# Hybrid SSM and attention layer on one core: the product tanh·z plus z made by VectorE instead of GpSimd

## The chip, the cores and the metric

One core of a Trainium2 chip runs the whole kernel in one launch. The metric is device time in microseconds (us). PE is the matrix engine (PEld its weight loads), DVE is VectorE, ACT is ScalarE, POOL is GpSimd, SP only issues DMAs. The five engines run their own instruction streams and meet by semaphores alone: a wait holds up everything that stands behind it on its own engine.

## The reference, cut to what matters

One layer of a streaming encoder works on 592 tokens (64 of a sample stream, 16 meta tokens, 512 of a prompt). A half-weight SwiGLU comes first, then one input projection that feeds a Mamba-2 branch and an attention branch, then their gated sum and a second SwiGLU. The change touches the gate of the Mamba-2 branch:

```python
P = u @ w_in            # columns: [SSD z | SSD x,B,C | dt | q | k | v | forget | gates]
...
y, final = ssd_chunked(xs, dt, a, bm, cm, ssm_init)      # chunked scan
y = y[:, front:front + L] + lw['d_skip'][:, None] * xs
y = y.reshape(b, L, D_SSM) * jax.nn.silu(z)              # the gate
yg = y.reshape(b, L, SSM_GROUPS, D_SSM // SSM_GROUPS)
yg = yg * lax.rsqrt(jnp.mean(yg * yg, axis=-1, keepdims=True) + EPS)
```

silu(z) is computed as 0.5 · (tanh(z/2) + 1) · z.

## The kernel before, in words

**Tiles.** The 592 tokens stand in five token tiles of 128, 128, 128, 128 and 80 rows. Every large product is made of three matmuls, since weights and activations are split into a rounded part (`wh`, `xah`) and a remainder (`wl`, `xal`). The weights come by DMA into `raw`; ACT rounds them to `wh`, and POOL makes `wl = raw - wh` (L798) in the stretch that matters here, in quarters of 128x512.

**Stages.** First SwiGLU, then the mixing stage (the change is there), then the output projection, the second SwiGLU and a final norm. The mixing stage has four iterations (`i` = 0 to 3) of two groups each (`g` = 0 and 1); one group is 256 columns of the Mamba-2 branch. Its input projection comes in pieces of 256 weight columns, in the order of the list `MID` = z, x, bc, z, x, bc, v, q0, q1, k. The first z belongs to g=0, the second to g=1.

**Order of the work.** There is no scheduler. One list of steps, written by hand, is shared by all engines: `FIRST_STEPS`, then `LOOP_STEPS` three times, then `LAST_STEPS`. Each engine has its own function `mid` that walks the list and does its part of every step. A step ("lin", n, t, ...) is PE's piece: token tile t of column piece n. It carries inner steps, placed between PE's 24 matmuls of the piece; `flat` hands an engine the inner steps first and the piece itself after them. So what DVE or POOL does for a piece stands in its stream behind what it does for the inner steps of that piece.

**Where the z pieces lie.** Five z tiles of g=0 open the stage (`FIRST_STEPS`, the "opening"). In each iteration the scan of g=0 (`ssd_window` with g=0: conv, then per token tile `s1`, `s1b`, `s2`) is run between the pieces z, x, bc of g=1, so the five z tiles of g=1 lie beside the scan of g=0. The scan of g=1 runs between v, q, k, with no z. In iterations 0 to 2 the attention heads (`heads_window`) run between the pieces z, x, bc of g=0 for the next iteration. That makes 5 + 4·5 + 3·5 = 40 z tiles.

**One z tile before the change.** PE makes the piece (`token_tile`, L1705); ACT evacuates it twice from PSUM: `zt` = tanh(z/2) and `zr` = z (L1076 and L1077 in the opening, L1079 and L1080 elsewhere), and raises `act_free`. Both have two buffers, so that ACT waits on `z_used` for the tile two back. POOL waits for `act_free` and makes `zt + 1` in place (L816), then `zs = zt · zr` (L817), and raises `z_used`. `zs` holds all five tiles of both groups; DVE reads it in `yg = 0.5 · y1 · zs` (L1586) at the end of a token tile's `s2`.

**DVE's part of the scan, by lines.** `s1`: four decay differences `eb` (L1539), which ACT turns into exponentials. `s1b`: `cbm` (L1546), the masked product C·B out of PSUM bank 5, and `mb` (L1550). `s2`: the states `sfin` or `spr` (L1563 to L1570), `y` (L1577, L1580, L1582), `yg` (L1586). PE writes C·B of the next token tile into the same bank (L1945), so that it waits until `cbm` of the tile before has been read:

```python
pe.wait_ge(cbm_ready, i * 10 + (PRIMED + tau))                       # s1 on PE
pe.matmul(bank(5, m, m), cv[:, 2, c], cv[:, 3, c], start=True, stop=True).then_inc(cb_ready, 1)
```

**The opening on DVE.** Eight norm products `full` (L1451) and eight remainders `xal` (L1455), in inner steps of the z pieces, then the small chain of the step sizes (L1461 to L1480) whose result `tstack` PE transposes (L1761).

**POOL's other work in the mixing stage** is `wl` (L798), the columns of the conv's history, and in `s1` the three products `xdd`, `xsk`, `xd` per token tile (L839).

Of the kernel before, what the change touches and what calls it, by code (L numbers as in the profile page):

```python
# [8 lines left out]
ALU = mybir.AluOpType  # L9
# [35 lines left out]
ROWS = [128, 128, 128, 128, TOK - 512]  # L45
# [63 lines left out]
PRIMED = 2  # L109


MID = ["z", "x", "bc", "z", "x", "bc", "v", "q0", "q1", "k"]
# [176 lines left out]
def freed(i, n, t):  # L289


    return i * MID_OUTS + (KT + 1 + OUT_AT[n] + t + 1)
# [28 lines left out]
def fox_ssd_hybrid_kernel(nc, x_prompt, x_sample, cache_k, cache_v, cache_logf, state_ssm, state_conv,  # L321
# [6 lines left out]
    with ctx:  # L328
# [80 lines left out]
        with ExitStack() as s:  # L409
# [12 lines left out]
            zt = sb("zt", [P, 2, 256], F32, s)  # L422
            zr = sb("zr", [P, 2, 256], F32, s)
            zs = sb("zs", [P, 2, TILES, 256], F32, s)
# [52 lines left out]
        hi_ready, split_done, key_split = sem("hi_ready"), sem("split_done"), sem("key_split")  # L477
        cleared = sem("cleared")
        lin_out, act_free, dve_free = sem("lin_out"), sem("act_free"), sem("dve_free")
        gated, full_ready, xhi_ready, x_ready = sem("gated"), sem("full_ready"), sem("xhi_ready"), sem("x_ready")  # L480
        sq_ready, sq_used, ss_ready, ss_summed = sem("sq_ready"), sem("sq_used"), sem("ss_ready"), sem("ss_summed")
        root_ready, rs_ready, a_ready, sc_ready = sem("root_ready"), sem("rs_ready"), sem("a_ready"), sem("sc_ready")
# [6 lines left out]
        z_used, hist_ready = sem("z_used"), sem("hist_ready")  # L489
        tap0_ready, taps_done, tanh_ready, cv_done = sem("tap0_ready"), sem("taps_done"), sem("tanh_ready"), sem("cv_done")  # L490
        brow_in, sraw_in, sraw_T, sini_ready = sem("brow_in"), sem("sraw_in"), sem("sraw_T"), sem("sini_ready")
        dec_ready, cst_T, cst_ready, cst_out = sem("dec_ready"), sem("cst_T"), sem("cst_ready"), sem("cst_out")
        xb_T, xb_ready, cb_ready, cbm_ready = sem("xb_T"), sem("xb_ready"), sem("cb_ready"), sem("cbm_ready")
        seg_ready, e_ready, m_ready, xd_ready = sem("seg_ready"), sem("e_ready"), sem("m_ready"), sem("xd_ready")
        xdd_ready = sem("xdd_ready")
        st_ready, s_ready, yo_ready, yd_ready = sem("st_ready"), sem("s_ready"), sem("yo_ready"), sem("yd_ready")
        y_used, yg_ready, sq_done, rv_ready = sem("y_used"), sem("yg_ready"), sem("sq_done"), sem("rv_ready")
# [6 lines left out]
        qk_ready, s_free, p_ready, p_T = (sem(n) for n in ("qk_ready", "s_free", "p_ready", "p_T"))  # L504
# [216 lines left out]
        def _(pool):  # L721
# [3 lines left out]
            def link(ins):  # L725
                ins.then_inc(gch, 1)
                pool.wait_ge(gch, chain.up())

            def settle():

                pool.sem_inc(passed, 1)

            pool.sem_inc(z_used, PRIMED)


            def input_half(n):

# [65 lines left out]
            def mid(now, steps):  # L803
                for step in flat(steps):
                    i, kind, g = now, step[0], step[1] if len(step) > 1 else 0
                    if kind == "split":
                        split_quarter(1 - MID_SLOT[g], step[2], split_cols(g), shared(g, step[2]))
                    if kind == "lin" and MID[g] == "z":

                        i, t, g = now + step[3], step[2], g // 3  # L810
                        if t == 0 and step[3]:
                            pool.wait_ge(yg_ready, now * 10 + (PRIMED + 5))
                        m, b = ROWS[t], (g + t) % 2
                        pool.wait_ge(act_free, freed(i, step[1], t))
                        settle()
                        link(pool.tensor_scalar(zt[0:m, b, :], zt[0:m, b, :], 1.0, None, ALU.add))  # L816
                        pool.tensor_tensor(zs[0:m, g, t, :], zt[0:m, b, :], zr[0:m, b, :], ALU.mult).then_inc(z_used, 1)  # L817
                    elif kind == "lin" and MID[g] == "x" and step[2] == 0:

                        i, g = now + step[3], g // 3  # L820
                        pool.wait_ge(taps_done, i * 8 + (PRIMED + 4 * g))
                        pool.wait_ge(cst_T, i * 2 + (PRIMED + g))
                        settle()
                        hist = par[:, PC_STATE:PC_STATE + 96].rearrange("p (r t) -> p t r", r=3)
                        pool.memset(xp[:, :, CS_ + SAMPLE:CP_], 0.0)
                        pool.tensor_copy(xp[:, 0:2, 0:3], hist[:, bass.ds(i * 4 + 2 * g, 2), :])
                        pool.tensor_copy(xp[:, 2:3, 0:3], hist[:, bass.ds(i * 2 + (16 + g), 1), :])
                        pool.tensor_copy(xp[:, 3:4, 0:3], hist[:, bass.ds(i * 2 + (24 + g), 1), :]).then_inc(hist_ready, 1)
                    elif kind == "s1":
                        t = step[2]  # L830
                        m, b, hs, tau = ROWS[t], (t + g) % 2, i * 8 + 4 * g, PRIMED + 5 * g + t
                        xv = xbt[0:m, b, 0:256].rearrange("p (h c) -> p h c", h=4)
                        pool.wait_ge(xb_ready, i * 10 + (tau + 1))
                        pool.wait_ge(yd_ready, i * 10 + (tau - 1))
                        pool.wait_ge(y_used, i * 10 + (tau - 1))


                        def by_column(dst, src):
                            return pool.tensor_tensor(dst[0:m, b, :].rearrange("p (h c) -> p h c", h=4), xv,  # L839
                                                      src.unsqueeze(2).to_broadcast([m, 4, HD]), ALU.mult)  # L840

                        by_column(xdd, tokt[0:m, t, bass.ds(hs + 64, 4)]).then_inc(xdd_ready, 1)
                        by_column(xsk, dsk[0:m, bass.ds(hs, 4)])
                        by_column(xd, tokt[0:m, t, bass.ds(hs + 32, 4)]).then_inc(xd_ready, 1)
                    elif kind == "fetch":
                        pool.wait_ge(ssd_left, i + 1)
                        settle()
                        pool.memset(pp[:, :, 0:SAMPLE], 0.0).then_inc(pz_ready, 1)
                    elif kind == "stage":
                        pool.wait_ge(heads_left, 4 + g)  # L850
                        settle()
                        k0, k1 = ((0, 3), (3, KT))[g]
                        to = 0
                        for c0, c1 in KEPT:
                            pool.dma_start(G2["h"][:, k0:k1, to:to + c1 - c0], oa_spill[k0:k1, :, c0:c1].rearrange("j p t -> p j t"))\
                                .then_inc(stage_in[g], 16)
                            to += c1 - c0
# [412 lines left out]
        def _(dve):  # L1270
# [2 lines left out]
            chain, full, xhi, nsplit = Count(), Count(), Count(), Count()  # L1273
            half = HALF

            for s in (split_done, dve_free, a_ready, full_ready, taps_done, cv_done, seg_ready, cbm_ready, m_ready, s_ready, y_used, yg_ready, s_free):
                dve.sem_inc(s, PRIMED)

            def link(ins):
# [136 lines left out]
            def stage(i, n):  # L1416

                k = n - 2
                if k >= 0:
                    hh, t = job(k)  # L1420
                    m = ROWS[t]
                    dve.wait_ge(pv_ready, i * JOBS + (k + 1))
                    link(dve.reciprocal(rinv[0:m, k % 4:k % 4 + 1], rsum[0:m, k % 4:k % 4 + 1]))
                    dve.tensor_scalar(otok[0:m, t, HD * hh:HD * hh + HD], bank(7, HD, m, at=256),
                                      rinv[0:m, k % 4:k % 4 + 1], None, ALU.mult).then_inc(o_ready, 1)
                if n < JOBS:
                    hh, t = job(n)
                    m, (before, w) = ROWS[t], score_span(t)
                    dve.wait_ge(bias_in[hh % 2], i * 96 + 48 * (hh // 2 + 1))
                    diagonal = bias[0:m, hh % 2, PAST:PAST + m] if t == 0 else bias[0:m, hh % 2, PAST + P + before:PAST + P + w]  # L1430
                    link(dve.tensor_tensor(diagonal, diagonal, negmask[0:m, min(t, 1), 0:m], ALU.add))
                    dve.wait_ge(qk_ready, i * JOBS + (n + 1))
                    if n >= 2:
                        dve.wait_ge(p_T, i * JOBS + (n - 1))
                    bs = bias[0:m, hh % 2, 0:PAST + P] if t == 0 else bias[0:m, hh % 2, PAST + P:PAST + P + w]
                    dve.sem_inc(met, 1)
                    dve.tensor_tensor_reduce(out=scores(t), in0=bank(4, w, m, at=BANK - before), in1=bs, scale=1.0, scalar=LEAST,
                                             op0=ALU.add, op1=ALU.min, accum_out=mx[0:m, n % 4:n % 4 + 1]).then_inc(s_free, 1)

            def mid(now, steps):  # L1440
                for step in flat(steps):
                    i, kind, g = now, step[0], step[1] if len(step) > 1 else 0
                    if kind == "half" and g % 2 == 0:
                        stage(i, g // 2)
                    elif kind == "norm":

                        if g < KT:
# [81 lines left out]
                    elif kind == "s1":  # L1529
                        t = step[2]  # L1530
# [549 lines left out]
```

## Time and profile before

| what | value |
|---|---|
| median of 3 runs | 2035.76 us (2035.05 to 2035.95) |
| profiled execution, its own time | 2037.11 us |
| its span | 2035.5 us |
| granted clock of PE | 0.994 of full speed |
| PE busy | 1980.0 us, 97% of the span |
| DVE busy | 988.7 us, 49% |
| ACT busy | 754.9 us, 37% |
| POOL busy | 425.7 us, 21% |

The profiled execution took 1.35 us more than the median of the runs; its span, from the first to the last instruction, is 1.6 us shorter than its own time. Shares of busy time are averages over stages that differ.

### The profile page before, as it was taken

The page shows a single profiled execution, that of the slowest core. Times are in us where ns is not written, and L with a number is a line of the kernel's source. Part 1 is how long each engine was busy: PE and PEld are TensorE (multiplying, and loading weights), DVE is VectorE, ACT ScalarE, POOL GpSimd, SP SyncE. Part 2 cuts the span into 40 slices and gives each one's busy share as a digit, 9 for nine tenths or more (in the row PEclk, how much of TensorE's full clock was granted, in tenths as well). Part 3 has the DMA queues.
Part 4 walks back from the last instruction along what each step waited for, and adds up shares of the span by engine and source line. Part 5 has one row for each costly group of instructions (what it writes and reads, how often), then busy time and mean ns, then how long its engine had stood idle before and what let it go on. Part 6 is the DMA issues. An engine that isn't in the chain of part 4 may idle for free. (4 is left out here: it accounts for less than half of the span.)

```text
span 2035.5 us, 36914 instructions
## 1 busy us (share of the span) xinstructions
PE 1980.0 (97%) x14807; PEld 1929.5 (95%) x14807; DVE 988.7 (49%) x1713; ACT 754.9 (37%) x1362; POOL 425.7 (21%) x516
## 2 busy tenths in 40 slices
PE   6999999998999999999999999999999999999997
PEld 6999999997899989998999899999999999999997
DVE  4433432457873477347735872214454543343344
ACT  5221221235455445554555454333223322222223
POOL 1000000005644264416442643223110000000000
PEclk9999999999999999999999999999999999999999
DMA  5222222213325222522261225315433222222222
GB/s 155 64 87 77 82 83 83 72 56 111 94 86 174 66 73 68 177 63 81 60 200 41 81 62 166 104 54 161 130 105 107 83 83 89 77 82 89 77 67 62
DMA packets 226657, 190.04 MB, mean 93 GB/s; under 512 B 10880, under 2 KB 214976, under 8 KB 225376
## 3 DMA queue, kind: packets, MB, share of 16 engines
q1 hardware_dynamic: 221568, 173.76, 28.4%
q0 software_dynamic: 4416, 14.32, 2.3%
q8 instruction: 88, 1.44, 0.3%
q14 instruction: 41, 0.34, 0.1%
q10 hardware_dynamic: 544, 0.17, 0.0%
HBM read 168.89 MB, written 19.33 MB: 92 GB/s over the span
## 5 line engine op out<-in xcount | busy, mean ns | idle before, releaser
L1693 PE MATMUL ps<-xah,wh 128*128 128x296 f32 (+1 forms) x2336 | 516.8, 302 | 6.9 <-DVE xal L1298 3.9
L1693 PE MATMUL ps<-xah,wl 128*128 128x296 f32 (+1 forms) x2336 | 515.4, 302 | 0.0
L1693 PE MATMUL ps<-xal,wh 128*128 128x296 f32 (+1 forms) x2336 | 510.2, 300 | 0.0
L1693 PEld LDWEIGHTS ps<-xah,wh 128*128 128x128 f32 x2336 | 378.4, 190 | 8.6 <-DVE xal L1298 3.5
L1693 PEld LDWEIGHTS ps<-xal,wh 128*128 128x128 f32 x2336 | 379.8, 189 | 0.0
L1693 PEld LDWEIGHTS ps<-xah,wl 128*128 128x128 f32 x2336 | 377.6, 189 | 0.1
L798 POOL TENSOR_TENSOR wl<-raw,wh 128x512 fp32r<-128x512 f32 (+1 forms) x184 | 231.4, 1265 | 412.5 <-ACT wh L917 412.5
L1693 PE MATMUL ps<-xbl,wh 128*128 128x288 f32 (+1 forms) x1312 | 282.6, 297 | 0.0
L1693 PE MATMUL ps<-xbh,wh 128*128 128x288 f32 (+1 forms) x1312 | 281.1, 295 | 1.1 <-DVE xbl L1292 1.1
L1693 PE MATMUL ps<-xbh,wl 128*128 128x288 f32 (+1 forms) x1312 | 280.7, 295 | 0.0
L909 ACT ACTIVATE wh<-raw 128x2048 fp32r<-128x2048 f32 x84 | 160.1, 1906 | 243.1 <-PE ps L1693 243.1
L1286 DVE TENSOR_TENSOR wl<-raw,wh 128x2048 fp32r<-128x2048 f32 x85 | 194.9, 2293 | 103.9 <-ACT wh L909 91.1
L1693 PEld LDWEIGHTS ps<-xbh,wl 128*128 128x128 f32 x1312 | 212.8, 190 | 0.0
L1693 PEld LDWEIGHTS ps<-xbh,wh 128*128 128x128 f32 x1312 | 210.6, 188 | 1.3 <-issue 1.3
L1693 PEld LDWEIGHTS ps<-xbl,wh 128*128 128x128 f32 x1312 | 209.7, 188 | 0.0
L1338 DVE TENSOR_TENSOR full<-ps,rs 128x592 f32<-128x592 f32 (+1 forms) x44 | 33.7, 766 | 225.2 <-PE ps L1693 225.1
L1705 PE MATMUL ps<-wh,xal 128*128 128x256 f32 (+1 forms) x440 | 128.0, 291 | 0.0
L1705 PE MATMUL ps<-wh,xah 128*128 128x256 f32 (+1 forms) x440 | 125.6, 285 | 1.2 <-ACT zr L1080 1.2
L1705 PE MATMUL ps<-wl,xah 128*128 128x256 f32 (+1 forms) x440 | 124.9, 284 | 0.0
L1327 DVE SCALAR_TENSOR_TENSOR h<-ps,h 128x592 f32 (+3 forms) x56 | 42.8, 764 | 159.1 <-PE ps L1693 158.9
L917 ACT ACTIVATE wh<-raw 128x512 fp32r<-128x512 f32 (+1 forms) x192 | 110.4, 591 | 0.2
L1511 DVE SCALAR_TENSOR_TENSOR cvt<-xp,parh,cvt 128x595 f32<-128x595 f32 x96 | 98.5, 1026 | 19.7 <-ACT cvt L1145 17.9
(273 smaller groups left out, 2438.9 us busy)
## 6 DMA issues: line engine op xcount, KB each, us to landing
raw<-in_ffn_w_in_dram SPq DMA_DIRECT2D x88, 512.0 KB, 5.0
raw<-in_w_in_dram SPq DMA_DIRECT2D x80, 512.0 KB, 4.7
raw<-in_ffn_w_out_dram SPq DMA_DIRECT2D x32, 512.0 KB, 4.0
brow<-acs_rows SPq DMA_DIRECT2D x8, 1184.0 KB, 6.7
raw<-in_w_br_ssm_dram SPq DMA_DIRECT2D x16, 512.0 KB, 4.0
raw<-in_ffn_w_out_dram SPq DMA_DIRECT2D x16, 384.0 KB, 3.5
bias<-bias_rows SPq DMA_DIRECT2D x32, 160.0 KB, 5.2
os_spill<-yT SPq DMA_DIRECT2D x8, 592.0 KB, 3.0
```

The source lines that it names most:

```text
L798: ins = pool.tensor_tensor(wl[:, slot, k, 0:cols], raw[:, slot, k, 0:cols], wh[:, slot, k, 0:cols].bitcast(F32), ALU.subtract)
L909: act.activation(wh[:, slot, :, 0:cols], raw[:, slot, :, 0:cols], ACT.Copy).then_inc(hi_ready, 1)
L917: act.activation(wh[:, slot, k, 0:cols], raw[:, slot, k, 0:cols], ACT.Copy).then_inc(hi_ready if c == 3 else hi_part, 1)
L1286: dve.tensor_tensor(wl[:, slot, :, 0:cols], raw[:, slot, :, 0:cols], wh[:, slot, :, 0:cols].bitcast(F32), ALU.subtract)\
L1327: dve.scalar_tensor_tensor(out=hm, in0=halves(b, half=half), scalar=0.5, in1=hm, op0=ALU.mult, op1=ALU.add)\
L1338: link(dve.tensor_tensor(in_halves(G["full"][:, n, :]), halves(4 * n + 2, half=half), rs, ALU.mult))
L1511: ins = dve.scalar_tensor_tensor(out=c, in0=xp[:, j, tap:tap + CO], scalar=parh[:, bass.ds(conv_tile(i, g, j) + 32 * tap, 1)], in1=c, op0= ...
L1693: ins = pe.matmul(bank(b + a, half), w[:, slot, k, j * P:(j + 1) * P], x[:, k, a * half:(a + 1) * half], start=(k == 0 and w is wh and x i ...
L1705: ins = pe.matmul(bank(b, 256, m), x[:, k, t * P:t * P + m], w[:, slot, k, :], start=(k == 0 and w is wh and x is xh), stop=(k == KT - 1 a ...
```

## The change

POOL no longer touches z. DVE makes `zs = (zt + 1) · zr` in one scalar_tensor_tensor per tile, in its own branch of `mid` for the z pieces, and raises `z_used`, which is now primed by DVE.

```diff
@@ POOL
-            pool.sem_inc(z_used, PRIMED)
...
-                    if kind == "lin" and MID[g] == "z":
-
-                        i, t, g = now + step[3], step[2], g // 3
-                        if t == 0 and step[3]:
-                            pool.wait_ge(yg_ready, now * 10 + (PRIMED + 5))
-                        m, b = ROWS[t], (g + t) % 2
-                        pool.wait_ge(act_free, freed(i, step[1], t))
-                        settle()
-                        link(pool.tensor_scalar(zt[0:m, b, :], zt[0:m, b, :], 1.0, None, ALU.add))
-                        pool.tensor_tensor(zs[0:m, g, t, :], zt[0:m, b, :], zr[0:m, b, :], ALU.mult).then_inc(z_used, 1)
-                    elif kind == "lin" and MID[g] == "x" and step[2] == 0:
+                    if kind == "lin" and MID[g] == "x" and step[2] == 0:
@@ DVE
-            for s in (split_done, dve_free, ..., s_free):
+            for s in (split_done, dve_free, ..., s_free, z_used):
                 dve.sem_inc(s, PRIMED)
...
                     if kind == "half" and g % 2 == 0:
                         stage(i, g // 2)
+                    elif kind == "lin" and MID[g] == "z":
+
+                        i, t, g = now + step[3], step[2], g // 3
+                        m, b = ROWS[t], (g + t) % 2
+                        if t == 0 and step[3]:
+                            dve.wait_ge(yg_ready, now * 10 + (PRIMED + 5))
+                        dve.wait_ge(act_free, freed(i, step[1], t))
+                        dve.scalar_tensor_tensor(out=zs[0:m, g, t, :], in0=zt[0:m, b, :], scalar=1.0, in1=zr[0:m, b, :],
+                                                 op0=ALU.add, op1=ALU.mult).then_inc(z_used, 1)
```

In the changed kernel the new instruction is L1440, and the DVE lines named above come 3 earlier in the file (L1539 is L1536 there). The order of POOL's remaining work, of PE's and of ACT's is the same.

**DVE in the opening, before** (norm products and remainders of the first steps; `rsb_ready` is the norm's root, `xhi_ready` ACT's rounded part):

```order
L1451 TENSOR_TENSOR full<-h,rs 128x592 [waits rsb_ready] x2
L1455 SCALAR_TENSOR_TENSOR xal<-full,par,xah 128x592 [waits xhi_ready]
L1451 TENSOR_TENSOR full<-h,rs 128x592 [waits x_ready,rsb_ready]
L1455 SCALAR_TENSOR_TENSOR xal<-full,par,xah 128x592 [waits xhi_ready]
L1451 TENSOR_TENSOR full<-h,rs 128x592 [waits x_ready,rsb_ready]
L1455 SCALAR_TENSOR_TENSOR xal<-full,par,xah 128x592 [waits xhi_ready]
```

The same place in the changed kernel:

```order
L1440 SCALAR_TENSOR_TENSOR zs<-zt,zr 128x256 [waits act_free]
L1448 TENSOR_TENSOR full<-h,rs 128x592 [waits rsb_ready] x2
L1452 SCALAR_TENSOR_TENSOR xal<-full,par,xah 128x592 [waits xhi_ready]
L1440 SCALAR_TENSOR_TENSOR zs<-zt,zr 128x256 [waits act_free]
L1448 TENSOR_TENSOR full<-h,rs 128x592 [waits x_ready,rsb_ready]
L1452 SCALAR_TENSOR_TENSOR xal<-full,par,xah 128x592 [waits xhi_ready]
L1440 SCALAR_TENSOR_TENSOR zs<-zt,zr 128x256 [waits act_free]
L1448 TENSOR_TENSOR full<-h,rs 128x592 [waits x_ready,rsb_ready]
```

A z product that waits for ACT now stands ahead of the first norm product, and one between each group of them.

**DVE in the scan of g=0 (one iteration), before**, from the end of the conv to the states of token tile 0 (`cv` is the conv's output, `m_ready` DVE's own earlier `mb`, `cb_ready` PE's C·B, `e_ready` ACT's exponentials, `st_ready` PE's states):

```order
L1526 SCALAR_TENSOR_TENSOR cv<-th,cvt 128x64 [waits tanh_ready]
L1526 SCALAR_TENSOR_TENSOR cv<-th,cvt 128x528
L1539 TENSOR_SCALAR eb<-brow,tokt 128x128 [waits m_ready,heads_left,brow_in]
L1539 TENSOR_SCALAR eb<-brow,tokt 128x128 x3
L1546 TENSOR_TENSOR cbm<-ps,mask 128x128 [waits cb_ready]
L1550 TENSOR_TENSOR mb<-eb,cbm 128x512 [waits yd_ready,e_ready,cbm_ready]
L1539 TENSOR_SCALAR eb<-brow,tokt 128x128 [waits m_ready]
L1539 TENSOR_SCALAR eb<-brow,tokt 128x128 x3
L1563 SCALAR_TENSOR_TENSOR sfin<-sini,dec,ps 128x64 [waits sini_ready,sf_T,dec_ready,st_ready]
```

The same place in the changed kernel:

```order
L1440 SCALAR_TENSOR_TENSOR zs<-zt,zr 128x256 [waits act_free]
L1523 SCALAR_TENSOR_TENSOR cv<-th,cvt 128x64 [waits tanh_ready]
L1523 SCALAR_TENSOR_TENSOR cv<-th,cvt 128x528
L1440 SCALAR_TENSOR_TENSOR zs<-zt,zr 128x256 [waits act_free]
L1536 TENSOR_SCALAR eb<-brow,tokt 128x128 [waits m_ready,heads_left,brow_in]
L1536 TENSOR_SCALAR eb<-brow,tokt 128x128 x3
L1543 TENSOR_TENSOR cbm<-ps,mask 128x128 [waits cb_ready]
L1547 TENSOR_TENSOR mb<-eb,cbm 128x512 [waits yd_ready,e_ready,cbm_ready]
L1440 SCALAR_TENSOR_TENSOR zs<-zt,zr 128x256 [waits act_free]
L1536 TENSOR_SCALAR eb<-brow,tokt 128x128 [waits m_ready]
L1536 TENSOR_SCALAR eb<-brow,tokt 128x128 x3
L1560 SCALAR_TENSOR_TENSOR sfin<-sini,dec,ps 128x64 [waits sini_ready,sf_T,dec_ready,st_ready]
```

The z products of token tiles 1 and 2 now stand ahead of the `eb` of token tiles 0 and 1, which waited for nothing of ACT's before; that of tile 0 stands ahead of the conv's last part.

## Rows read from the trace of the kernel before

**Rows 1.** The page's first part: busy time of each engine, share, instructions.
```profile
PE 1980.0 (97%) x14807; PEld 1929.5 (95%) x14807; DVE 988.7 (49%) x1713; ACT 754.9 (37%) x1362; POOL 425.7 (21%) x516
```
**Rows 2.** PE's waits, whole span: line, what it waited for, us, times, longest.
```profile
PE ps L1945 <- DVE cbm L1546: 7.7, 8, 1.4
PE ps L1761 <- DVE tstack L1480: 5.8, 1, 5.8
PE ps L1693 <- POOL wl L798: 3.0, 1, 3.0
```
**Rows 3.** Single lines: duration in ns (min/median/max), first and last start in us.
```profile
L816 POOL TENSOR_SCALAR zt<-zt x40: 843/856/1372, 475.3 to 1151.7; 128x256 f32<-128x256 f32 x32, 80x256 f32<-80x256 f32 x8
L817 POOL TENSOR_TENSOR zs<-zt,zr x40: 724/733/984, 476.3 to 1152.7; 128x256 f32<-128x256 f32 x32, 80x256 f32<-80x256 f32 x8
L1586 DVE SCALAR_TENSOR_TENSOR yg<-y,zs x40: 420/572/1945, 543.6 to 1222.5; 128x256 f32<-128x256 f32 x32, 80x256 f32<-80x256 f32 x8
L1582 DVE TENSOR_TENSOR y<-y x40: 420/442/1011, 542.9 to 1222.0; 128x256 f32<-128x256 f32 x32, 80x256 f32<-80x256 f32 x8
```
**Rows 4.** Scans of g=0, g=1: us; busy PE, PEld, DVE, ACT, POOL; clock; DMA; GB/s.
```profile
526.76:576.36 49.60, 46.27 (x347) 43.09 (x345) 40.15 (x94) 25.92 (x63) 29.55 (x38) 1.00 0.25 76
586.66:632.70 46.04, 45.45 (x347) 43.07 (x346) 35.26 (x90) 23.18 (x56) 19.86 (x26) 1.00 0.27 81
```
**Rows 5.** The opening: two lines' durations, then timeline rows (start, us; idle before).
```profile
L1451 DVE TENSOR_TENSOR full<-h,rs x8: 764/954/1680, 473.0 to 489.8; 128x592 f32<-128x592 f32 x8
L1455 DVE SCALAR_TENSOR_TENSOR xal<-full,par,xah x8: 833/1324/1872, 475.8 to 491.4; 128x592 fp32r<-128x592 f32 x8
...
472.99 2.18 DVE L1451 TENSOR_TENSOR full<-h,rs 128x592 f32<-128x592 f32 x2 [5.66 <-ACT rs L1109]
490.49 2.24 DVE L1455 SCALAR_TENSOR_TENSOR xal<-full,par,xah 128x592 fp32r<-128x592 f32 x2
474.65 0.47 ACT L1077 ACTIVATE zr<-ps,rcol 128x256 f32<-128x256 f32 x1
```
**Rows 6.** Timeline of DVE, scan of g=0, iteration 0.
```profile
534.18 1.02 DVE L1539 TENSOR_SCALAR eb<-brow,tokt 128x128 f32<-128x128 f32 x4
536.21 0.29 DVE L1546 TENSOR_TENSOR cbm<-ps,mask 128x128 f32<-128x128 f32 x1 [1.02 <-PE ps L1945]
538.05 2.49 DVE L1539 TENSOR_SCALAR eb<-brow,tokt 128x128 f32<-128x128 f32 x4
541.05 0.85 DVE L1563 SCALAR_TENSOR_TENSOR sfin<-sini,dec,ps 128x64 f32<-128x64 f32 x4 [0.51 <-PE ps L1965]
544.28 0.28 DVE L1546 TENSOR_TENSOR cbm<-ps,mask 128x128 f32<-128x128 f32 x1
545.41 2.31 DVE L1539 TENSOR_SCALAR eb<-brow,tokt 128x128 f32<-128x128 f32 x4
```
**Rows 7.** Timeline of ACT and POOL beside it.
```profile
535.50 0.36 ACT L1080 ACTIVATE zr<-ps 128x256 f32<-128x256 f32 x1
536.90 0.63 ACT L917 ACTIVATE wh<-raw 128x512 fp32r<-128x512 f32 x1
538.50 0.38 ACT L1080 ACTIVATE zr<-ps 128x256 f32<-128x256 f32 x1
...
535.82 1.28 POOL L798 TENSOR_TENSOR wl<-raw,wh 128x512 fp32r<-128x512 f32 x1
```
**Rows 8.** Timeline of PE beside it: C·B of token tiles 2, 3 and 4.
```profile
544.74 0.39 PE L1945 MATMUL ps<-cv 128*128 128x128 f32 x2
550.65 0.49 PE L1945 MATMUL ps<-cv 128*128 128x128 f32 x2 [0.52 <-DVE cbm L1546]
557.06 0.37 PE L1945 MATMUL ps<-cv 128*80 128x80 f32 x2 [1.38 <-DVE cbm L1546]
```
**Rows 9.** Heads window of iteration 0: busy times as in rows 4, DVE's longest wait.
```profile
642.90:726.50 83.60, 83.21 (x650) 77.40 (x649) 37.37 (x113) 44.32 (x105) 23.65 (x26) 1.00 0.39 117
DVE bias L1431 <- DMA bias<-biasp_rows: 22.1, 1, 22.1
```

More of the change, by code:

```diff
@@ L1274, in _ @@
             half = HALF
-            for s in (split_done, dve_free, a_ready, full_ready, taps_done, cv_done, seg_ready, cbm_ready, m_ready, s_ready, y_used, yg_ready, s_free):
+            for s in (split_done, dve_free, a_ready, full_ready, taps_done, cv_done, seg_ready, cbm_ready, m_ready, s_ready, y_used, yg_ready, s_free, z_used):
                 dve.sem_inc(s, PRIMED)
```

## Prediction, made before the changed kernel was run

> **What bounds the kernel now.** The busy times come first: PE works 97% of the span, DVE 49%, POOL 21% [rows 1]. Neither DVE nor POOL bounds the whole; either can cost time only where PE waits for it. So the second view is PE's waits [rows 2]. Two of them belong to DVE streams that the change alters: 7.7 us on `cbm` before C·B (L1945, 8 waits, up to 1.4 us) and 5.8 us on `tstack` at the end of the opening. One 3.0 us wait on POOL's `wl` lies in the opening too, ahead of the one on `tstack`; whatever is won there is waited again, so it counts nothing.
>
> The third view is the windows [rows 4]. The scan of g=0, with the z pieces of g=1 beside it, lasts 49.60 us; the scan of g=1, with no z, 46.04. Its PE work is the same in number (347 matmuls each). The difference of 3.56 us is what z with its company costs today in one scan, and there are four of them. PE is idle 49.60 - 46.27 = 3.33 us in the first, 0.59 us in the second. The rest of the argument is about the order of DVE's stream there.
>
> The fourth is the durations [rows 3, 5]. An instruction of DVE with two inputs in SBUF has a steady shortest time and a wide spread: `yg` 420 ns alone, up to 1945. `eb` took 1.02 us for four in one place and 2.49 and 2.31 in two others [rows 6]; POOL ran `wl` or products at those two places, z's 843 and 724 ns among them. So the two engines hold each other up, and POOL's z costs DVE time although DVE does not do it.
>
> **The change part by part.** Durations are from the profiled execution.
>
> *POOL's 80 instructions go*: 40 x (0.856 + 0.733) = 63.6 us of POOL [rows 3]. POOL is 21% busy [rows 1], so the time itself is worth nothing. What it gives is less contention on DVE, counted below.
>
> *DVE gets 40 fused products.* The nearest row is `yg`, the same form and size: 0.42 us alone [rows 3]; 40 x 0.42 = 16.8 us. A rule of the Trainium skill speaks against that: Vector Engine (DVE) Microarchitecture Reference, section Points that are easy to get wrong, says that scalar_tensor_tensor with two SBUF sources that aren't bf16 runs at half throughput. The trace does not bear it out: `yg` in this form has the same shortest time as the plain tensor_tensor `y`, 420 ns for 256 elements [rows 3]. By the rule, with the streaming part of 256 elements doubled, the product would be about 0.7 us, 0.28 x 5 = 1.4 us more per scan and some 7 us over all.
>
> *The semaphores* (`z_used` raised by DVE, primed by it): nothing; ACT waits for the tile two back, a whole piece of 24 matmuls earlier. The `yg_ready` wait for the first tile is on DVE's own earlier work: nothing.
>
> *The opening, 5 tiles.* DVE starts its norm products at 472.99 today and ends the last remainder at 490.49 + 2.24 = 492.73 [rows 5]: 19.7 us for 8 + 8 instructions whose shortest times add up to 8 x 0.764 + 8 x 0.833 = 12.8 us [rows 5]. The 6.9 us between are port waits and one wait on ACT. With the change the first product waits for ACT's `zr`, which ends at 474.65 + 0.47 = 475.12; it ends at about 475.6, so the chain starts 2.6 us later. Then come 12.8 us, four more products of 0.42 (1.7 us), and the stretching that stays, W. The end is 475.6 + 12.8 + 1.7 + W = 490.1 + W. With W as today (6.9) that is 497.0, or +4.3; with W = 2.0 it is 492.1, or -0.6. POOL's z falls away but its `wl` quarters stay, and each later product stands at a place where ACT has just evacuated, about 1 us each. I take W = 4.1, so **+1.5 us**. PE waits 5.8 us at the end of this chain [rows 2], so all of it counts.
>
> *The scan of g=0, four times.* Five products stand in DVE's stream, and two of them ahead of work on the way to PE:
> - That of token tile 1 stands ahead of the first `eb`. Today `eb` starts at 534.18, before `zr` of tile 1, which ends at 535.50 + 0.36 = 535.86 [rows 6, 7]. POOL's `wl` starts at 535.82 and runs 1.28 us, to 537.10 [rows 7]. So the product ends at about 537.5 and `eb` at 538.5 with 1.0 us of its own, not at 535.20: **3.3 us late**.
> - ACT's exponential stands behind it, and behind that the `wh` quarter (today 536.90) and the evacuation of z tile 2 (today 538.50) [rows 7]. ACT had some slack there; they slip by about 1.6 to 2.2 us, so `zr` of tile 2 is ready near 540.7, its product at 541.2.
> - The second `eb` follows. It takes 2.49 us today, with POOL's z and other products beside it [rows 6]; I take 2.1 us, so its end is 543.3, not 540.54. `sfin`, today at 541.05, starts at about 543.2: **2.1 us late** [rows 6].
> - From there DVE is packed until the C·B of tile 4: `cbm` of tile 1 (today 544.28) comes at about 546.4, and PE's C·B of tile 2, at 544.74 today without a wait, waits for it, some 1.9 us. For tiles 3 and 4 PE waits 0.52 and 1.38 today [rows 8], behind the same chain.
> - Given back: the `eb` of tile 2 takes 2.31 us today [rows 6] and has no POOL z beside it after the change, about 1.0 us less; against it stands one more product. A product costs 0.42 and POOL's z of one tile held the port 1.6 us, so per tile up to 0.5 us comes back. From tile 2 to the 1.38 us wait of tile 4 that leaves about 1.1 us of the 2.1.
>
> So **+1.1 us per scan, +4.4 us in all**. The bounds: if the whole 3.56 us by which this window is longer went away and only the late start of 2.1 us came in, -1.5 us per scan, -6; if nothing were given back and a further wait for ACT stood in tile 3, +3 us per scan, +12.
>
> *The heads windows, 15 tiles.* DVE is busy 37.4 of 83.6 us, and its one long wait, 22.1 us, is on a DMA [rows 9]. PE is busy 83.21 of the 83.60. The products are hidden in DVE's idle time: **0**. If that cover were gone it would be 15 x 0.42 = 6.3 us.
>
> **Sum:** 1.5 + 4.4 + 0 = +5.9 us. The profiled execution took 2037.1 us, so 2043.0. It stood 1.35 us above the median of the runs; on the median the forecast is **2041.7 us**, 0.3% slower. About 0.2%, 4.1 us, is what a measurement of this kernel can tell from no change.
>
> **The rivals.**
> 1. *No change that can be told.* The late `eb` is absorbed: DVE's first `cbm` waits 1.02 us for PE today [rows 6], and the chain from tile 1 to tile 4 makes the loss up at 0.5 us per tile or more. Then +0.3 us per scan and +0.5 in the opening, 1.7 us in all: 2037.5. For it: PE's idle time in the scan is 3.33 us and only waits on `cbm` tie it to this chain [rows 4, 8]. Against it: PE's waits on `cbm` grow already today from tile 3 to tile 4, so DVE does not make time up there.
> 2. *Faster: the port binds the scan of g=0.* DVE is busy 40.15 us there against 35.26 without z, though it does four instructions more [rows 4]: some 4 us of its stretching are POOL's doing. If that is the cause of the 1.38 us wait, freeing the port shortens every token tile by more than the late start costs: -1.5 us per scan, -0.6 in the opening, 2029.2. It decides at the second `eb`: this case holds if it ends before about 541 and `cbm` of tile 1 starts no later than 544.6. For it: the tile periods of DVE's packed stretch hold 1.3 us of stretched `eb`. Against it: the first `eb` has to wait for `zr`, whatever the port does. By itself: the Trainium skill, GPSIMD Engine Reference, section Engine selection, puts additions and products of a tile on VectorE, GpSimd being about twice as slow with two inputs. The rows agree on the price (724 against 420 ns), but the rule says nothing of the place in the stream.
> 3. *Clearly slower: the products wait for ACT at every tile.* ACT evacuates z behind an exponential that itself waits for DVE's `eb`, so that the two engines alternate and nothing is given back: +2.5 us per scan and +3 in the opening, 13 us: 2048.8. For it: two of the products stand right behind such evacuations. Against it: from tile 3 on, ACT's evacuation comes before DVE reaches the place.
> That the change doesn't do what it says is no case: the 40 instructions stand in DVE's stream, and POOL's are gone.
>
> **How the numbers follow.** The forecast (+2.5 to +9 us, centre +5.9) 0.48, rival 1 0.27, rival 2 0.15, rival 3 0.10. The range takes in the forecast, rival 1 and the nearer half of each of the outer two: 2032.0 to 2048.5. Slower by over 0.2% is nearly all of the forecast (0.44) with rival 3 (0.10), 0.54; within 0.2% is rival 1 (0.27) with the forecast's low end (0.04), 0.31; faster 0.15.
>
> **What the profile would show.** Right: PE's wait on `tstack` grows from 5.8 to about 7.3 us; the g=0 window grows from 49.60 to about 50.7 while the g=1 window stays at 46.04; the first `eb` of a scan starts about 3 us later in it, behind a product that waited for `zr`; waits on `cbm` rise from 7.7 to about 12 us and appear at tile 2; the product's shortest time is 0.42 us; the heads windows stay as they are. Wrong: a g=0 window under 49 us (rival 2), a product of 0.7 us (the page's rule), growing heads windows (then DVE's idle time there was no cover), or a granted clock below today's in the scans.

## The result: slower by 0.7%, nearly all of it in the scans of g=0

| | median of the runs | profiled execution | span | granted clock |
|---|---|---|---|---|
| before (6 runs) | 2035.78 us (2035.05 to 2036.37) | 2037.11 | 2035.5 | 0.994 |
| changed (6 runs) | 2049.82 us (2047.85 to 2052.35) | 2050.47 | 2048.9 | 0.991 |

The ratio is 1.0067, 95% interval [1.0057, 1.0077]: 14 us slower, in the direction of the forecast (+5.9) but above its range. The page's first part of the changed kernel, to be read against [rows 1]:

```profile
PE 1985.9 (97%) x14807; PEld 1933.8 (94%) x14807; DVE 996.0 (49%) x1753; ACT 755.4 (37%) x1362; POOL 360.4 (18%) x436
```

POOL lost 65 us (63.6 forecast). DVE gained 7, less than the 16.8 of its products, so its other work took some 9 us less. But PE, whose 14807 matmuls are the same, is busy 5.9 us longer. Its waits, against [rows 2]:

```profile
PE ps L1942 <- DVE cbm L1543: 14.6, 8, 1.9
PE ps L1758 <- DVE tstack L1477: 7.3, 1, 7.3
PE ps L1690 <- POOL wl L796: 1.3, 1, 1.3
```

The wait on `tstack` grew by the 1.5 us that were forecast; those on `cbm` by 6.9. The windows of the two scans of iteration 0, in the columns of [rows 4]:

```profile
527.54:580.42 52.88, 48.01 (x347) 44.61 (x345) 41.01 (x99) 25.93 (x63) 21.77 (x27) 0.97 0.23 71
590.71:636.80 46.09, 45.47 (x347) 43.13 (x346) 35.28 (x90) 23.18 (x56) 19.83 (x26) 1.00 0.27 81
```

The scan of g=1 has not changed. The scan of g=0 takes 52.88 us against 49.60: 3.28 us more, where 1.1 were forecast. PE's idle time there is 52.88 - 48.01 = 4.87 us against 3.33, +1.5; its busy time is 48.01 against 46.27, +1.7, and the clock column has fallen to 0.97. The other three scans of g=0 grew as much (the table in the third set of runs).

The timeline of DVE in that scan:

```profile
534.75 0.42 DVE L1440 SCALAR_TENSOR_TENSOR zs<-zt,zr 128x256 f32<-128x256 f32 x1 [1.31 <-ACT zr L1068]
536.68 0.67 DVE L1440 SCALAR_TENSOR_TENSOR zs<-zt,zr 128x256 f32<-128x256 f32 x1 [0.75 <-ACT zr L1068]
537.27 1.98 DVE L1536 TENSOR_SCALAR eb<-brow,tokt 128x128 f32<-128x128 f32 x4
...
541.01 1.09 DVE L1440 SCALAR_TENSOR_TENSOR zs<-zt,zr 128x256 f32<-128x256 f32 x1 [0.32 <-ACT zr L1068]
542.02 1.97 DVE L1536 TENSOR_SCALAR eb<-brow,tokt 128x128 f32<-128x128 f32 x4
543.91 0.84 DVE L1560 SCALAR_TENSOR_TENSOR sfin<-sini,dec,ps 128x64 f32<-128x64 f32 x4
...
547.57 0.28 DVE L1543 TENSOR_TENSOR cbm<-ps,mask 128x128 f32<-128x128 f32 x1
...
549.35 0.86 DVE L1536 TENSOR_SCALAR eb<-brow,tokt 128x128 f32<-128x128 f32 x4
...
554.01 2.15 DVE L1536 TENSOR_SCALAR eb<-brow,tokt 128x128 f32<-128x128 f32 x4
...
559.65 0.28 DVE L1543 TENSOR_TENSOR cbm<-ps,mask 128x128 f32<-128x128 f32 x1
```

The scan began 0.8 us later than before (PE's first transpose of the conv's output at 536.22, before at 535.43), so 0.8 is to be taken off. The first `eb` ends at 537.27 + 1.98 = 539.25 (before 535.20): 3.3 us late, as forecast. Behind it ACT's `zr` of tile 2 is ready at 540.98 (before 538.88), 1.3 us late where 1.8 were forecast. `sfin` starts 543.91 - 541.05 - 0.8 = 2.1 us late, as forecast. `cbm` of tile 1 starts 547.57 - 544.28 - 0.8 = 2.5 us late. PE's side, C·B of tiles 2, 3 and 4 as in [rows 8]:

```profile
547.90 0.49 PE L1942 MATMUL ps<-cv 128*128 128x128 f32 x2 [1.86 <-DVE cbm L1543]
553.24 0.39 PE L1942 MATMUL ps<-cv 128*128 128x128 f32 x2
559.99 0.47 PE L1942 MATMUL ps<-cv 128*80 128x80 f32 x2 [1.83 <-DVE cbm L1543]
```

C·B of tile 2 now waits 1.86 us, that of tile 4 1.83 instead of 1.38. What follows the second wait is in the windows of 1 us (columns as in [rows 4]; the clock is the third from the end):

```profile
557.00:558.00 1.00, 1.00 (x10) 0.88 (x8) 0.96 (x3) 0.35 (x1) 0.57 (x1) 1.00 0.00 0
558.00:559.00 1.00, 0.15 (x2) 0.00 (x0) 0.98 (x1) 0.49 (x1) 0.95 (x2) 1.00 0.00 0
559.00:560.00 1.00, 0.01 (x1) 0.01 (x1) 0.95 (x3) 0.00 (x0) 1.00 (x2) 1.00 0.00 0
560.00:561.00 1.00, 1.00 (x5) 1.00 (x6) 0.96 (x2) 0.00 (x0) 1.00 (x2) 0.56 0.00 0
561.00:562.00 1.00, 1.00 (x4) 0.82 (x3) 0.79 (x4) 0.17 (x1) 0.22 (x1) 0.50 0.06 16
562.00:563.00 1.00, 1.00 (x5) 0.82 (x5) 0.22 (x2) 1.00 (x4) 0.00 (x0) 0.50 0.00 0
563.00:564.00 1.00, 1.00 (x8) 1.00 (x8) 0.64 (x4) 0.21 (x1) 0.71 (x1) 0.74 0.67 208
```

PE idles, and then, for some 3.5 us, its clock is granted at the lower level, 1.2 GHz, with half the matmuls to the microsecond. The shares missing add up to 0.44 + 0.50 + 0.50 + 0.26 = 1.7 us. Each of the four scans of g=0 has one such stretch in the changed kernel; none has one before.

The theory to be tested: the product is cheap, its **place** is not. It makes DVE wait for ACT ahead of work that PE waits for, and the longer waits bring the clock down. The main rival: it is the **price**, DVE having no room for five more instructions in a scan, wherever they stand.

### The profile page after: what moved, and what is told of

Same layout as the page of the kernel before. It is cut to its first block and busy times, and to the rows that moved or that the text cites. A ratio compares the mean times of both kernels' runs of the same rounds, so it can differ in the third digit from the quotient of the medians.

```text
span 2048.9 us, 36834 instructions
## 1 busy us (share of the span) xinstructions
PE 1985.9 (97%) x14807; PEld 1933.8 (94%) x14807; DVE 996.0 (49%) x1753; ACT 755.4 (37%) x1362; POOL 360.4 (18%) x436
## 3 DMA queue, kind: packets, MB, share of 16 engines
q1 hardware_dynamic: 221568, 173.76, 28.1%
```

## The experiments

### First set: which of the three places, and the same work one piece later

Three kernels make only the z tiles of one place on DVE, those of the others on POOL as before. The edit is against the kernel before; `on_dve` returns `steps is FIRST_STEPS` for the opening, `step[1] == 3` for the scans and `step[3] == 1` for the heads:

```diff
@@ POOL
-                    if kind == "lin" and MID[g] == "z":
+                    if kind == "lin" and MID[g] == "z" and not on_dve(now, step, steps):
...
@@ DVE
+                    elif kind == "lin" and MID[g] == "z" and on_dve(now, step, steps):
...
```

> Only the five z tiles of the opening are made by DVE, the other 35 by POOL as before. Place theory (a product that waits for ACT stands ahead of DVE's work on the way to PE): the chain up to tstack ends about 1.5 us later, PE's wait on tstack 7 to 7.5 us against 5.8; net about +1.5 us, 2037.3; the scans stay at 49.60 us with full granted clock. Price theory (DVE has no room for the products wherever they stand): 5/40 of the loss of 14 us, about +1.8 us. The two agree here; the run sizes the opening.

Measured: 2038.13 us against 2036.07 before on the same chip, ratio 1.0011 [1.0002, 1.002]: +2.1 us. PE waits 7.3 us on `tstack`.

> Only the 20 z tiles beside the scans of g=0 are made by DVE, the others by POOL as before. Place theory: nearly all of the loss, four times 3.3 us, about 2049 us; each scan of g=0 52.9 us long against 49.60, with about 1.5 us more idle time of PE and a stretch of some 3.5 us at half the granted clock. Price theory: half of the products, half of the loss, about 2043.

Measured: 2048.93 us, ratio 1.0061 [1.0048, 1.0075]: +12.9 us, with four stretches at half clock.

> Only the 15 z tiles beside the attention heads are made by DVE. Place theory: no change within 0.5 us of before (2035.8), since DVE waits there for DMA and PE. Price theory: 15/40 of the loss, about +5 us, 2041.

Measured: 2036.13 us, ratio 1.0 [0.9991, 1.0009]: no change that can be told. The three add up to 15.0 us, about the 14 of the whole. An equal share per product, as the simple price theory has it, is out: 20 products cost 12.9 us, 15 others nothing.

The fourth kernel keeps all 40 products on DVE, each one piece later in its stream (this edit and those that follow are against the changed kernel, but for `before_fill`):

```diff
-                    elif kind == "lin" and MID[g] == "z":
...
+                    elif kind == "lin":
+                        for held_now, held in late_z:
+                            z_product(held_now, held)      # the wait and the product as in the change
+                        late_z[:] = [(now, step)] if MID[g] == "z" else []
```

> All 40 tiles on DVE in the fused form, but each product stands one piece later in DVE's stream (behind the inner steps of the next piece), where ACT's evacuation has long ended. Same number of instructions and same price. Place theory: the scans' waits on cbm fall to those of before or below (7.7 us or less), no stretch at half clock in a scan, and the opening's chain starts as early as before: 2030 to 2036.5 us, that is as fast as before or a little faster since POOL's 1.6 us per tile no longer hold DVE up. Price theory: still 2045 to 2050.

Measured: 2034.48 us, ratio 0.9992 [0.9983, 1.0001]. The 14 us are gone with no product less. Its waits on `cbm` are under those of before, and its C·B of tiles 2 and 4 in iteration 0:

```profile
PE ps L1948 <- DVE cbm L1549: 6.6, 8, 1.1
```

```profile
542.60 0.49 PE L1948 MATMUL ps<-cv 128*128 128x128 f32 x2 [0.61 <-DVE cbm L1549]
...
554.24 0.37 PE L1948 MATMUL ps<-cv 128*80 128x80 f32 x2 [1.06 <-DVE cbm L1549]
```

So the place decides. That POOL's 64 us were taken off and the time hardly fell is not explained by this run; the third set shows it.

### Second set: which product, the clock, and the price

> The changed kernel, but beside the scans the products of token tiles 0 and 1 stand one piece later in DVE's stream; tiles 2 to 4, the opening and the heads stand as in the change. If the products ahead of the conv's last part and of the first eb are what counts (DVE's first eb starts 2.6 us later into the scan, ACT's evacuation of tile 2 slips behind it), the second product finds zr of tile 2 ready near its old time, C·B of tile 2 waits less than 1 us and the clock holds: 2036 to 2039 us, of which about 2 are the opening's. If the product ahead of the second eb is what counts, 2045 or more.

```diff
+def is_late(step):
+    return step[1] == 3 and step[2] in (0, 1)     # z_t2_late: step[2] == 2
```

Measured: 2042.78 us, ratio 1.0034 [1.0021, 1.0048], above what was expected. Tile 1's late place is the place where tile 2's product stands in the change, so both stand ahead of the second `eb`, one behind the other:

```profile
538.68 2.23 DVE L1440 SCALAR_TENSOR_TENSOR zs<-zt,zr 128x256 f32<-128x256 f32 x2
540.84 1.97 DVE L1548 TENSOR_SCALAR eb<-brow,tokt 128x128 f32<-128x128 f32 x4
```

The two products took 2.23 us there, against 0.84 for two at their shortest, while POOL ran its products and `wl` beside them; and two of the four scans kept the stretch at half clock.

> The changed kernel, but beside the scans the product of token tile 2 alone stands one piece later. If the first eb's lateness is what counts: it stays about 2.6 us late, so the time falls only by what the second eb no longer waits for zr of tile 2 (some 0.3 us in each scan), 2045 to 2049 us. If the product ahead of the second eb is what counts: 2036 to 2040.

Measured: 2046.87 us, ratio 1.0052 [1.0038, 1.0066], as expected where the first `eb` counts. Neither move alone is enough. The second one does not shorten the waiting at all: where the clock held, a scan lasts 42.65 us, as long as the changed kernel's without the clock's fall (the table below). What it won came from two scans in which the clock did not fall.

The clock by itself:

```diff
                         ins.then_inc(xb_T, 1)
+                        if g == 0 and t in (2, 4):
+                            for _ in range(6):
+                                pe.matmul(bank(3, P, m), cv[:, 2, c], cv[:, 3, t * P - P:t * P], start=True, stop=True)
                         pe.wait_ge(cbm_ready, i * 10 + (PRIMED + tau))
```

> The changed kernel with six more 128x128 matmuls on PE ahead of its wait on cbm, at token tiles 2 and 4 of each scan of g=0 (48 in all, into a PSUM bank that nobody reads there), so that PE is busy for most of the two gaps of 1.9 us; everything else, and every wait, is the same. Theory that the idle gaps bring the granted clock down: the four stretches of some 3.5 us at half clock go, 4 x 1.7 = about 6.5 us, 2043 to 2044.5. Theory that the clock falls for something else, or that the whole loss is waiting: 2049 to 2051, no change or slower by what the extra matmuls take.

Measured: 2044.29 us, ratio 1.0042 [1.0028, 1.0056]: 5.5 us less than the changed kernel (the ratios 1.0067 and 1.0042 differ by 0.0025, 5.1 us), by adding work to PE. Its timeline of PE and two windows at the same place:

```profile
545.60 1.50 PE L1943 MATMUL ps<-cv 128*128 128x128 f32 x12
547.62 0.49 PE L1945 MATMUL ps<-cv 128*128 128x128 f32 x2 [0.52 <-DVE cbm L1543]
...
557.74 1.47 PE L1943 MATMUL ps<-cv 128*80 128x128 f32 x12
559.71 0.37 PE L1945 MATMUL ps<-cv 128*80 128x80 f32 x2 [0.50 <-DVE cbm L1543]
```

```profile
559.00:560.00 1.00, 0.50 (x5) 0.30 (x4) 0.97 (x3) 0.00 (x0) 1.00 (x3) 1.00 0.00 0
560.00:561.00 1.00, 1.00 (x8) 0.92 (x7) 0.96 (x3) 0.00 (x0) 0.94 (x1) 1.00 0.00 0
```

PE gets to C·B of tile 2 as late as without the filling (547.62 - 535.94 = 11.68 us after the scan's first transposes of `cv`, in the changed kernel 547.90 - 536.22 = 11.68), so DVE's lateness is the same; but the clock stays at 1.00 in all scans. So the clock is a cost of its own, and the idle gaps are its cause.

The price by itself: `z_late` with each of the 20 products beside the scans done twice.

```diff
+                if step[1] == 3:
+                    link(dve.scalar_tensor_tensor(out=zdup[0:m, :], in0=zt[0:m, b, :], scalar=1.0, in1=zr[0:m, b, :],
+                                                  op0=ALU.add, op1=ALU.mult))
                 dve.scalar_tensor_tensor(out=zs[0:m, g, t, :], ...
```

> As z_late (2034.5), but beside the scans each of the 20 products is done twice, the first into a scratch tile that DVE waits for. Place theory (at a late place the price is hidden): within 2 us of z_late, 2034 to 2036.5. Price theory (each 0.4 to 0.5 us that DVE does more in a scan is paid by PE): 20 x 0.5 = +10 us, 2044.

Measured: 2041.8 us, ratio 1.0027 [1.0016, 1.0038]: 7 us over `z_late`. The place theory had it hidden; it is not. At these places a scan has no free room on DVE for more products: five more of them cost 42.57 - 41.03 = 1.5 us (the table below).

### Third set: without the products, a better place, and the clock of the opening

```diff
+                if step[1] == 3:
+                    dve.sem_inc(z_used, 1)
+                    return
                 dve.scalar_tensor_tensor(out=zs[0:m, g, t, :], ...
```

> As z_late, but the 20 products beside the scans are left out on every engine (zs of g=1 stays at a constant), so that neither DVE nor POOL does anything for them. If a late product is hidden in DVE's idle time, nothing changes: 2034 to 2035. If DVE's part of the scan is full and every product there is paid by PE's wait on cbm, also at a late place, as the doubled products (+7 us for 20 of them) say: about 2029, bounded by the 6.6 us of cbm waits that z_late still has.

Measured: 2027.61 us against 2037.15 before on this chip, ratio 0.9951 [0.9938, 0.9965], 9.5 us. PE no longer has a wait on `cbm`. Against `z_late` the ratios differ by 0.0041, 8.3 us, more than the 6.6 us of waits that were taken for the bound.

To compare the kernels without the opening, here is one scan of g=0 by itself, from PE's first transpose of the conv's output (`cv`) to its transposes of `yg`. For the kernel before, the changed one, `z_late` and `z_none`, in iteration 0, these are the two rows:

```profile
535.43 0.52 PE L1761 MATMUL ps<-ident,cv 128*128 128x128 f32 x3 [0.37 <-issue]
...
576.37 1.24 PE L1761 MATMUL ps<-ident,yg 128*128 128x128 f32 x10 [0.39 <-DVE yg L1602]
```

```profile
536.22 0.52 PE L1758 MATMUL ps<-ident,cv 128*128 128x128 f32 x3 [0.36 <-DVE cv L1523]
...
580.42 1.24 PE L1758 MATMUL ps<-ident,yg 128*128 128x128 f32 x10 [0.39 <-DVE yg L1599]
```

```profile
532.51 0.52 PE L1764 MATMUL ps<-ident,cv 128*128 128x128 f32 x3 [0.36 <-issue]
...
573.53 1.24 PE L1764 MATMUL ps<-ident,yg 128*128 128x128 f32 x10 [0.40 <-DVE yg L1605]
```

```profile
532.73 0.52 PE L1768 MATMUL ps<-ident,cv 128*128 128x128 f32 x3 [0.36 <-issue]
...
571.75 1.24 PE L1768 MATMUL ps<-ident,yg 128*128 128x128 f32 x10 [0.42 <-DVE yg L1609]
```

The same distance in all four scans of each kernel:

| kernel | us, four scans | against before |
|---|---|---|
| before | 40.94 | |
| changed | 44.18 to 44.24 | +3.3 |
| changed, gaps filled | 42.68 | +1.7 |
| tiles 0, 1 late | 41.93, 41.94 and 43.40, 43.46 | +1.0, with the clock's fall +2.5 |
| tile 2 late | 42.65, 42.67 and 44.17, 44.20 | +1.7, with the clock's fall +3.2 |
| all late | 41.02 to 41.04 | +0.1 |
| all late, twice | 42.56 to 42.59, one 44.12 | +1.6, with the clock's fall +3.2 |
| left out | 39.02 to 39.11 | -1.9 |
| z_mid (below) | 40.60 | -0.3 |

So a scan's +3.3 us comes apart, by differences of two rows each: POOL's z gone, -1.9; five products on DVE at a place without a wait, 41.03 - 39.06 = +2.0, that is 0.4 us each, about the duration of one; the place, 42.68 - 41.03 = +1.65; the clock, 44.2 - 42.68 = +1.5.

The place can be better still. `z_mid` is `z_late` with the products of tiles 0 and 1 between the first `cbm` and the first `mb`; that of tile 0 is held over the piece of tile 1 for it:

```diff
+                        if not (g == 3 and step[2] == 1):
+                            for held_now, held in late_z:
+                                z_product(held_now, held)
+                            late_z[:] = []
...
                         dve.tensor_tensor(cbm[0:m, 0:m], bank(5, m, m), ...).then_inc(cbm_ready, 1)
+                        if tau == 0:
+                            for held_now, held in late_z:
+                                z_product(held_now, held)
+                            late_z[:] = []
                         dve.wait_ge(cbm_ready, i * 10 + (PRIMED + tau + 1))
```

> z_late, but the products of token tiles 0 and 1 of each scan stand between the first cbm and the first mb, where DVE waits about 0.55 us for ACT's exponential, instead of ahead of the first and the second eb. If what stands ahead of an eb is what PE pays for, 0.4 to 0.8 us less per scan: 2031.5 to 2033. Rival, the order among the late places doesn't matter: 2034.5.

Measured: 2033.45 us, ratio 0.9982 [0.9973, 0.9991], 3.7 us faster than the 2037.15 of the kernel before on this chip: the place with a wait of 0.55 us that was there anyway hides half of the price of two products (40.60 against 41.03 in the table). This kernel is faster than the one before and the changed one.

Two kernels fill PE's wait on `tstack` in the opening, since a stretch at half clock follows that too, before and after the change:

```diff
                     elif kind == "t4":
+                        for _ in range(22):
+                            pe.matmul(bank(7, P), ident[:, :], ident[:, :], start=True, stop=True)
                         pe.wait_ge(t_dve, 3)
```

> The kernel before with 22 further 128x128 matmuls of ident on PE in the opening, ahead of its wait of 5.8 us on tstack, into a bank that nobody reads there; z stays with POOL. Clock theory: the stretch of 10 us at half the granted clock behind that wait goes, 5.1 us less, about 2031. Rival, that the clock falls there for another reason: 2036.

Measured: 2032.57 us, ratio 0.9977 [0.9968, 0.9986], 4.6 us less.

> z_late with 26 further matmuls ahead of the wait on tstack and 3 ahead of C·B of token tile 4 in the scans of g=0. The stretch at half clock behind the opening's wait goes: 2034.5 - 5.1 = 2029.4, range 2028.5 to 2031. Rival, no change: 2034.5.

Measured: 2031.97 us, ratio 0.9975 [0.9965, 0.9984]: 5.2 us less than before, where 6.7 were expected (1.6 of `z_late` and 5.1). The filling was too short: PE still waited 1.5 us on `tstack`, and some 3.5 us at the lower level were left behind that wait, a third of what `z_late` has there. Its three further matmuls at tile 4 changed nothing that can be told: its scans last 41.02 to 41.04 us, as those of `z_late`.

```profile
PE ps L1764 <- DVE tstack L1483: 1.5, 1, 1.5
```

One window of a microsecond behind the opening's wait, in the kernel before and in `before_fill`:

```profile
509.00:510.00 1.00, 1.00 (x4) 0.69 (x5) 0.95 (x4) 0.44 (x1) 0.04 (x1) 0.50 0.00 0
```

```profile
509.00:510.00 1.00, 1.00 (x10) 1.00 (x9) 0.96 (x4) 0.28 (x2) 0.00 (x0) 1.00 0.15 16
```

## Why the prediction was too low, point by point

The step that failed is "+1.1 us per scan". It priced a wait of PE at its length alone and left out what the clock costs behind it, 1.5 to 1.7 us per scan and some 6 in all; the waiting itself it put too low by 0.4 us per scan. Point by point:

- **The opening, +1.5 forecast:** right. The wait on `tstack` went from 5.8 to 7.3 us, and the opening alone measured +2.1 us [0.4, 4.1]. Here are the norm's root on ACT, with which the chain begins, and PE's first transpose of `tstack` behind it, in the kernel before, the changed one and `z_late`:

```profile
472.31 0.65 ACT L1109 ACTIVATE rs<-ps 128x592 f32<-128x592 f32 x1
506.16 0.48 PE L1761 MATMUL ps<-ident,tstack 128*128 128x128 f32 x1 [5.77 <-DVE tstack L1480]
```

```profile
471.21 0.65 ACT L1097 ACTIVATE rs<-ps 128x592 f32<-128x592 f32 x1
506.51 0.47 PE L1758 MATMUL ps<-ident,tstack 128*128 128x128 f32 x1 [7.29 <-DVE tstack L1477]
```

```profile
471.75 0.64 ACT L1097 ACTIVATE rs<-ps 128x592 f32<-128x592 f32 x1
503.78 0.47 PE L1764 MATMUL ps<-ident,tstack 128*128 128x128 f32 x1 [7.30 <-DVE tstack L1483]
```

The distance is 33.85, 35.30 and 32.03 us: the chain is 1.45 us longer in the change and 1.8 shorter with the same products one piece later, so the place decides in the opening too. Since the scans of `z_late` last as long as before, the little that it wins is won there. The 1.7 us that PE won on `wl` came to nothing, as said: its wait on `tstack` begins 28.0 us behind the root in the changed kernel, 28.1 before.
- **The heads windows, 0 forecast:** right, 0.1 us measured.
- **The price of a product, 0.42 us:** right. Its shortest time in the changed kernel is 412 ns, its median 426:

```profile
L1440 DVE SCALAR_TENSOR_TENSOR zs<-zt,zr x40: 412/426/1094, 474.0 to 1163.8; 128x256 f32<-128x256 f32 x32, 80x256 f32<-80x256 f32 x8
```

By the rule of half throughput (the Trainium skill, Vector Engine (DVE) Microarchitecture Reference, Points that are easy to get wrong) it would have been some 0.7 us, by the prediction's estimate; the trace does not agree, with its 412 ns.
- **The late `eb`, 3.3 us, and `sfin`, 2.1 us:** right to a tenth, with their cause: the two products wait 0.75 and 0.32 us for `zr`, and ACT's evacuation of tile 2 slips by 1.3 us.
- **"From tile 2 to the 1.38 us wait of tile 4 that leaves about 1.1 us of the 2.1":** too low. C·B of tile 2 came 547.90 - 544.74 - 0.8 = 2.4 us late and that of tile 4 559.99 - 557.06 - 0.8 = 2.1, so 0.2 us came back instead of 1.0. DVE's packed stretch, from `cbm` of tile 1 to `cbm` of tile 3, for which C·B of tile 4 waits, took 556.73 - 544.28 = 12.45 us before and 559.65 - 547.57 = 12.08 after:

```profile
551.45 1.22 DVE L1539 TENSOR_SCALAR eb<-brow,tokt 128x128 f32<-128x128 f32 x4
...
556.73 0.28 DVE L1546 TENSOR_TENSOR cbm<-ps,mask 128x128 f32<-128x128 f32 x1
```

The `eb` of tile 2 fell from 2.31 to 0.86 us, more than was taken, but that of tile 3 rose from 1.22 to 2.15: ACT made the input of POOL's products later (`xbt` at 553.53 us, before 551.38), and these three (L839, now L827) ran beside it. In idle time of PE the error is small: 1.5 us per scan against 1.1.
- **A term that was missing:** the clock. The sum held no price for PE's gaps beyond their length; the text only listed a lower clock among what would prove it wrong. It is 1.5 to 1.7 us per scan, some 6 in all, over two fifths of the loss. With it and the measured 1.5 us of idle time the sum is 1.5 + 4 x (1.5 + 1.7) = 14.3 us; measured 14.0. One scan lost 3.3 us, more than even the outer bound of +3, whose condition, a further wait for ACT, did not come. The profile before could have warned: in it a stretch at half clock follows the wait of 5.8 us on `tstack`, and a shorter one, from 487 to 491 us, the wait of 3.0 us on `wl`.
- **Rival 1** is out: of the late start 0.2 us came back, not all of it.
- **Rival 2, the port, was half right.** POOL's z gone is worth 1.9 us per scan (the outer bound had taken 3.56 for it), but the five products cost 2.0 on DVE: an even exchange at the best, unless a wait hides a product, as in `z_mid`. That the scan decides at the second `eb` was right; it ended at 544.0 in the changed kernel, 543.2 without the later start, not under 541.
- **Rival 3** came nearest in time, 2048.8, for another reason: the waits for ACT at tiles 3 and 4 did not come (0.18 us at one of them), and the clock stood in for them. That its time was near is luck.

What stays open: when the clock falls. In the changed kernel it falls behind the first gap of a scan in some iterations and behind the second in others (from 751 us in iteration 1, from 560 in iteration 0, where the scans begin 203 us apart). Nor does the length of a gap settle it. With tiles 0 and 1 late, with tile 2 late and with all products late and done twice, each of the twelve scans has a wait of 1.0 to 1.2 us and then one of 2.12 to 2.15, and the clock fell behind the second in five of them. These two are of one kernel, `z_late_twice`, in iterations 2 and 3; the clock held behind the first, and behind the second it was at the lower level until 1167 us:

```profile
959.53 0.37 PE L1952 MATMUL ps<-cv 128*80 128x80 f32 x2 [2.14 <-DVE cbm L1553]
...
1161.19 0.37 PE L1952 MATMUL ps<-cv 128*80 128x80 f32 x2 [2.15 <-DVE cbm L1553]
```

## What to carry to other kernels

Work that waits for another engine is costed by what stands behind it in its own stream, and not by its duration alone: the same 40 instructions were worth +14 us at one place, next to nothing (-1.6, at the edge of the noise) one piece later, and -3.7 with two per scan in a wait that was there anyway. On an engine that is full in one stage and idle over all (49% here), look at the stage: in the scan five products cost 2.0 us and five more 1.5. And where PE is the bound, a gap costs more than its length once the granted clock falls behind it, so read the clock of the stretch behind each wait before a new wait is called cheap.

## What the runs showed of the hardware that had not been expected

A wait of 1.38 us (with one of 0.52 us 6 us earlier) left the clock at 1.00 in every scan before; two waits of 1.86 and 1.75 to 1.83 us 12 to 14 us apart, in the changed kernel, brought some 3.5 us at the lower level in every scan; one of 1.0 to 1.2 and one of 2.1 us, in three other kernels, did so in five scans of twelve. Matmuls whose result nobody reads, put into those gaps, kept the clock up and won 5 us though PE did more work; 22 of them in the opening's wait won 4.6 us in the kernel before.
